# Paired heads on the two column halves of TensorE in the 64-wide attentions of a two-block transformer kernel

## What is computed

```python
# first block, for each of 8 query heads h (two key/value heads, four query heads on each)
o_cmp = softmax(q_h @ kc.T) @ vc          # 31 compressed keys
o_slc = softmax(q_h @ k_slc.T + alibi_h) @ v_slc   # causal; the selection takes in every block here
o_win = softmax(q_h @ k_win.T + alibi_h) @ v_win   # causal; the window is as long as the sequence
o_nsa = g0 * o_cmp + g1 * o_slc + g2 * o_win
# second block, for each of 8 heads, one shared key and value head
o = softmax(where(selected, q_h @ k.T + bias_h, -inf)) @ v     # v is 512 x 64
```

## Time and profile before

| what | us |
|---|---|
| median of 3 runs | 1196.96 |
| span of the profiled execution, first to last instruction | 1194.5 |
| median less span (what lies around it) | 2.5 |
| PE busy | 1142.2 (96% of the span) |
| POOL, DVE, ACT busy | 496.7, 470.4, 470.3 |
| mean granted TensorE clock | 0.986 |

### The profile page before, as it was taken

One profiled execution on the slowest core, in us unless ns is written; L12 is line 12 of the kernel. 1 busy time (PEld: TensorE's weight loads), 2 busy tenths in 40 slices (PEclk: granted clock), 3 DMA queues, 4 the chain that ended last, 5 costly groups with the idle time before them and its releaser, 6 DMA issues.

```text
span 1194.5 us, 13900 instructions
## 1 busy us (share of the span) xinstructions
PE 1142.2 (96%) x5380; PEld 910.6 (76%) x5380; DVE 470.4 (39%) x971; ACT 470.3 (39%) x776; POOL 496.7 (42%) x222
## 2 busy tenths in 40 slices
PE   5999999898999989999999899998999999999996
PEld 4777778676776877788888678887888888878785
DVE  3574410387743231893520593713000000024544
ACT  6322332577765352522332673325212221223333
POOL 4331344654543523144434583442344434434441
PEclk9999999989999999999999899999999999999998
DMA  6324422000000623132332102232332332232321
GB/s 218 106 71 141 122 83 94 1 1 1 1 2 1 211 63 106 36 102 76 105 106 97 45 2 71 71 106 71 106 97 79 105 105 85 90 105 74 120 71 71
DMA packets 82480, 96.14 MB, mean 80 GB/s; under 512 B 8056, under 2 KB 66640, under 8 KB 82424
## 3 DMA queue, kind: packets, MB, share of 16 engines
q1 hardware_dynamic: 81864, 93.27, 24.6%
q0 software_dynamic: 560, 2.12, 0.5%
HBM read 93.26 MB, written 2.12 MB: 80 GB/s over the span
## 4 chain that ended last, share of the span: by engine, by line
PE 88%; DMA 3%; DVE 2%; ACT 2%; issue 2%; POOL 1%; SPq 1%; DVEq 0%; ACTq 0%; POOLq 0%
PE bank L1397 47%; PE bank L1454 21%; PE bank L1541 5%; PE bank L1500 5%; PE bank L1521 3%; DMA raw<-in_w_in 3%; PE bank L1650 1%; PE bank L1414 1%; PE bank L1478 1%; PE bank L1613 1%; POOL w_lo L627 1%; SPq L572 1%; PE bank L1576 1%; PE bank L1539 1%; PE bank L1533 1%
## 5 line engine op out<-in xcount | busy, mean ns | idle before, releaser
L627 POOL TENSOR_TENSOR w_lo<-raw,w_hi 128x2048 fp32r<-128x2048 f32 (+3 forms) x59 | 263.8, 4472 | 423.8 <-ACT w_hi L721 423.8
L1397 PE MATMUL bank<-h_hi,w_hi 128*128 128x512 f32 (+2 forms) x904 | 354.4, 392 | 1.5 <-POOL w_lo L627 1.4
L1397 PE MATMUL bank<-h_hi,w_lo 128*128 128x512 f32 (+2 forms) x904 | 352.0, 389 | 0.0
L1397 PE MATMUL bank<-h_lo,w_hi 128*128 128x512 f32 (+2 forms) x904 | 352.0, 389 | 0.0
L1397 PEld LDWEIGHTS bank<-h_hi,w_hi 128*128 128x128 f32 (+2 forms) x904 | 169.3, 187 | 39.0 <-POOL w_lo L627 1.8
L1397 PEld LDWEIGHTS bank<-h_lo,w_hi 128*128 128x128 f32 (+2 forms) x904 | 169.3, 187 | 36.3 <-issue 1.0
L1397 PEld LDWEIGHTS bank<-h_hi,w_lo 128*128 128x128 f32 (+2 forms) x904 | 169.3, 187 | 35.8
L721 ACT ACTIVATE w_hi<-raw 128x2048 fp32r<-128x2048 f32 (+3 forms) x59 | 109.8, 1861 | 208.4 <-PE bank L1454 138.5
L701 POOL TENSOR_TENSOR w_lo<-raw,w_hi 128x2048 fp32r<-128x2048 f32 x22 | 101.3, 4606 | 147.7 <-ACT w_hi L980 74.2
L1454 PE MATMUL bank<-w_hi,h_hi 128*128 128x512 f32 x368 | 144.6, 393 | 4.9 <-DVE h_lo L1269 2.5
L1454 PE MATMUL bank<-w_hi,h_lo 128*128 128x512 f32 x368 | 143.8, 391 | 0.0
(11 more groups left out here) (175 smaller groups left out, 1155.2 us busy)
## 6 DMA issues: line engine op xcount, KB each, us to landing
raw<-in_w_in SPq DMA_DIRECT2D x31, 1024.0 KB, 5.3
raw<-in_w_ffn_gate SPq DMA_DIRECT2D x11, 1024.0 KB, 5.3
raw<-in_w_ffn_up SPq DMA_DIRECT2D x11, 1024.0 KB, 5.3
raw<-in_w_out SPq DMA_DIRECT2D x8, 1024.0 KB, 5.1
raw<-in_w_ffn_down SPq DMA_DIRECT2D x8, 1024.0 KB, 5.0
raw<-in_cmp_w SPq DMA_DIRECT2D x4, 1024.0 KB, 5.7
raw<-in_w_ffn_down SPq DMA_DIRECT2D x4, 768.0 KB, 4.4
xres<-in_x SPq DMA_DIRECT2D x4, 512.0 KB, 4.9
```

Of the source, the lines that this page charges most:

```text
L627: nc.gpsimd.tensor_tensor(w_lo[:, s % 2, 0:size], raw[:, u.n % 2, 0:size], w_hi[:, s % 2, 0:size].bitcast(F32), ALU.subtract).then_inc(lo_ ...
L1397: ins = mm(dst, w_pair[w], h_pair[h], start=start and p == 0, stop=stop and p == 2)
```

## The change

The jobs of two heads of a group alternate: job 2m is of the even head and job 2m + 1 of the odd head, with the same branch and tile. In `nsa` a group is now compressed, compressed, then for each branch w = 1, 1, 2, 2, 3, 3, 4, 4. In `dsa` it is w = 1, 1, 2, 2, 3, 3, 4, 4.

PE issues the value products of a pair together, one matmul of the even head (output partitions 0 to 63) and one of the odd head (64 to 127) in turn, at the step where those of the second job stood. Those of the first job move one step back. The ring `PT` has a name for its size and keeps its three slots. PE asks for the stacks of two heads at a time, at steps 0, 8, 16 and 24 of `dsa`, and ACT's early split waits for the logits of a whole group. `diff` keeps its order.

```diff
+PRING = 3
...
-                for h in range(NSA_HEADS):
-                    kv = h // GROUP
-                    jobs.append(dict(g=h // 2, i=NT - 1, h=h, br=-1, subs=[], v=[vc[:, kv, :]]))
-                    for br in range(2):
-                        for i in range(NT):
...
+                for g in range(NSA_HEADS // 2):
+                    kv = 2 * g // GROUP
+                    for h in (2 * g, 2 * g + 1):
+                        jobs.append(dict(g=g, i=NT - 1, h=h, br=-1, subs=[], v=[vc[:, kv, :]]))
+                    for br, i, h in itertools.product(range(2), range(NT), (2 * g, 2 * g + 1)):
...
-                for h in range(DSA_HEADS):
-                    for i in range(NT):
+                for g, i in itertools.product(range(DSA_HEADS // 2), range(NT)):
+                    for h in (2 * g, 2 * g + 1):
...
-                    sc.wait_ge(s_done, attention["dsa"][NT * m + NT - 1]["r"] + 1)
+                    sc.wait_ge(s_done, attention["dsa"][2 * NT * (m // 2) + 2 * NT - 1]["r"] + 1)
...
-                            rows = slice(DH * (job["h"] % 2), DH * (job["h"] % 2) + DH)
-                            if not job["subs"]:
-                                ins = mm(O[rows, :], job["v"][0], pt, start=True, stop=False, skip_group_check=True)
-                            for j in range(i + 1 if job["subs"] else 0):
-                                ins = mm(O[rows, P * i:P * i + P], job["v"][j], pt[:, P * j:P * j + P],
...
+                    if 0 <= k - lag - 2 and which != "diff" and (k - lag) % 2 == 1:
+
+                        two = jobs[k - lag - 3:k - lag - 1]
+                        i, G = two[0]["i"], two[0]["G"]
+                        O = bank[O_BANKS[G % 2]]
+                        pe.wait_ge(pt_done, two[1]["n"] + 1)
...
+                        for j in range(1 if compressed else i + 1):
+                            for half, job in enumerate(two):
+                                rows, pt = slice(DH * half, DH * half + DH), PT[:, job["n"] % PRING, :]
+                                if compressed:
+                                    ins = mm(O[rows, :], job["v"][0], pt, start=True, stop=False, skip_group_check=True)
+                                else:
+                                    ins = mm(O[rows, P * i:P * i + P], job["v"][j], pt[:, P * j:P * j + P],
+                                             start=which == "dsa" and j == 0, stop=j == i and (which == "dsa" or job["br"] == 1),
+                                             skip_group_check=True)
+                                if j == i or compressed:
+                                    ins.then_inc(pv_done, 1)
...
-                if k in (0, 4):
-                    pe.wait_ge(first_stacks_done, 2 + k // 4)
-                elif k % 4 == 0 and k < len(attention["dsa"]):
-                    pe.wait_ge(stack_lo_done, stacked("dsa", 2 + k // 4))
+                if k == 0:
+                    pe.wait_ge(first_stacks_done, 3)
+                elif k % 8 == 0 and k < len(attention["dsa"]):
+                    pe.wait_ge(stack_lo_done, stacked("dsa", 3 + k // 4))
```

More of the change, by code:

```diff
@@ L1 @@
+import itertools
 import math
@@ L275, in build @@
         L = sb("L", [P, LRING, T])
-        PT = sb("PT", [P, 3, T])
+        PT = sb("PT", [P, PRING, T])
         st = sb("st", [P, 256])
@@ L475, in jobs_of @@
                                      select=pm_of(i))]
-                        jobs.append(dict(g=h // 2, i=i, subs=subs, h=h, br=0, v=[v2[:, j, :] for j in range(i + 1)]))
+                        jobs.append(dict(g=g, i=i, subs=subs, h=h, br=0, v=[v2[:, j, :] for j in range(i + 1)]))
             return jobs
@@ L833, in attend @@
                         sc.wait_ge(tr_done, n + 1)
-                        if n >= 3:
-                            sc.wait_ge(pv_done, n - 2)
-                        act_fn(PT[0:rows, n % 3, 0:w], t_bank(n)[0:rows, 0:w], ACT.Copy).then_inc(pt_done, 1)
+                        if n >= PRING:
+                            sc.wait_ge(pv_done, n - PRING + 1)
+                        act_fn(PT[0:rows, n % PRING, 0:w], t_bank(n)[0:rows, 0:w], ACT.Copy).then_inc(pt_done, 1)
                     if which == "diff" and 0 <= k - lag - 2 and jobs[k - lag - 2]["last"]:
@@ L1523, in attend @@
                         ins.then_inc(tr_done, 1)
-                    if 0 <= k - lag - 2:
+                    if 0 <= k - lag - 2 and which == "diff":
                         job = jobs[k - lag - 2]
-                        i, G, pt = job["i"], job["G"], PT[:, job["n"] % 3, :]
+                        i, G, pt = job["i"], job["G"], PT[:, job["n"] % PRING, :]
                         O = bank[O_BANKS[G % 2]]
@@ L1530, in attend @@
                             pe.wait_ge(o_free, G - 1)
-                        if which == "diff":
-                            for j in range(i + 1):
-                                ins = mm(O[:, P * i:P * i + P], pt[:, P * j:P * j + P], job["v"][j], start=j == 0,
-                                         stop=j == i)
-                        else:
-                            rows = slice(DH * (job["h"] % 2), DH * (job["h"] % 2) + DH)
-                            if not job["subs"]:
-                                ins = mm(O[rows, :], job["v"][0], pt, start=True, stop=False, skip_group_check=True)
-                            for j in range(i + 1 if job["subs"] else 0):
-                                ins = mm(O[rows, P * i:P * i + P], job["v"][j], pt[:, P * j:P * j + P],
-                                         start=which == "dsa" and j == 0, stop=j == i and (which == "dsa" or job["br"] == 1),
-                                         skip_group_check=True)
@@ L1544, in attend @@
-                        ins.then_inc(pv_done, 1)
+                        for j in range(i + 1):
+                            ins = mm(O[:, P * i:P * i + P], pt[:, P * j:P * j + P], job["v"][j], start=j == 0,
+                                     stop=j == i)
+                        ins.then_inc(pv_done, 1)
+                    if 0 <= k - lag - 2 and which != "diff" and (k - lag) % 2 == 1:
[3 more added lines that the diff above has]
+                        pe.wait_ge(pt_done, two[1]["n"] + 1)
+                        if G >= 2 and (k - lag - 3 == 0 or jobs[k - lag - 4]["last"]):
+                            pe.wait_ge(o_free, G - 1)
+                        compressed = not two[0]["subs"]
+                        for j in range(1 if compressed else i + 1):
[9 more added lines that the diff above has]
+                                    ins.then_inc(pv_done, 1)
```

8 lines of the change are left out of this document (4 added, 4 removed).

## The result

The changed kernel takes 1178.56 us (median of 4 runs, 1175.75 to 1184.13) against 1197.74 us (4 runs, 1196.86 to 1200.04) for the kernel before on the same chip: ratio 0.984, 95% interval 0.982 to 0.986. The direction was forecast, the size was not: 19 us instead of 29, and the time is 0.6 us above the range of 1156 to 1178.

The account below looks back on a forecast made before the run. PE was taken to bound nsa, with DVE and POOL nearly full in most of dsa. Savings of 25.4 us in nsa and 4 in dsa, 29.4 together, gave 1167.5 us against 1196.96, range 1156 to 1178.

Parts of the forecast that it names:

- What bounds: PE bounds nsa until ACT's or DVE's work is reached; in dsa DVE and POOL are nearly full.
- Streaming: Paired heads' value products overlap fully on column halves: PE saves 17.6 us in nsa, 8.8 in dsa, compressed products 3.6.
- only neighbours overlap: Rival for value products: strict program order leaves each pair one step more than half; 1172.5 us, chance 0.12.
- Entering and leaving: Halving the blocks of value products saves their 0.34 us of gaps each: 12.2 us in nsa, 5.4 in dsa.
- nsa by group: Each nsa group set by its fullest engine plus about 1 us of waits: 80.2 us instead of 105.6, saving 25.4.
- The ring: ACT's copy into PT waits for the pair's block; its 0.85 us fits while ACT is under 0.6 us behind.
- dsa: Saves 4 us, mainly in the last stretch with PE alone, ending near 719 instead of 723.5 us; bounds 0 to 8.
- The lost clock: Rival: PE's new pauses lower its clock through dsa and lose the gain there; 1171.5 us, chance 0.03.
- The signs: Pairs take 0.7 us (w = 2) and 1.1 (w = 4), nsa 86, dsa 49; ACT or DVE fullest in nsa's first two groups.
- No overlap: Rival: column halves share what they need, only gaps go, 12.2 us in nsa, about 3 in dsa; 1182 us, chance 0.06.
- PE as the bound: Rival: ACT and DVE fill their gaps without loss, saving 33.4 + 7 us; 1156.5 us, chance 0.08.
- The ping-pong: Rival: late ACT makes pair, copy and next pair follow one another, 52 us lost against 47.6 gained; 1201 us, chance 0.04.

Follow-up runs that it names:

- e3: Changed kernel with a pair's two inner loops swapped, so all of one head's records come before the other's; 1180.3 us, nsa 93.7 us.
- e4: Changed kernel with both heads of a pair put on columns 0 to 63, loops still alternating; 1192.3 us, nsa 104.1 us.
- e6: Changed kernel with DVE's bias addition in dsa (L1148) left out; 1165.0 us, dsa 42.6 us.
- e7: Changed kernel with POOL's early low parts and its stacks of heads 3 to 7 narrowed to 8 columns; 1173.1 us, dsa 48.2 us.
- e9: Kernel before the change with DVE's bias addition in dsa left out; 1193.9 us, dsa 48.8 us.
- e15: Changed kernel with the normalisation reordered: root behind the last exponential, DVE's pieces spread, same output; 1173.7 us, nsa 85.2 us.
- e8: Changed kernel with DVE's pieces of the normalisation behind the first attention narrowed to 8 columns; 1170.5 us, nsa 83.8 us.

## Why the prediction was right and wrong, step by step

**What bounds.** Right for `nsa`: all of the gain is there, and where PE bounds the third group it fell by 8.0 us. For `dsa` "two engines that are nearly full" was read rightly from the earlier trace rows but not carried through to the end of the stage.

**Streaming.** Right. Full overlap was chosen from L1551 against L1561, and the sixteen records take 1.09 us as forecast. The rule of the Trainium skill (TensorE: Matmul & The Clock Gate, "The mechanism" of packing small matmuls), that matmuls start and end in program order, stood behind the rival in which only neighbours overlap (chance 0.12). By it e3, where only two records of a pair are neighbours on different halves, should have been nearly as long as e4: some 1.85 us for sixteen. It took 1.58, and 0.66 where e4 took 1.09. The traces don't agree with the rule for these products.

**Entering and leaving.** Right where PE bounds: 3.1 us forecast for a group, 2.9 to 3.0 measured with e4 in the second and third.

**nsa by group.** Forecast 21.3, 21.8, 19.6 and 17.5 us, 80.2 in all; measured 23.8, 22.0, 18.9 and 18.6, 83.3. This is the step that failed in `nsa`. The second group was right (DVE's 20.6 us and a little more). For the first I took ACT's 20.5 us of work as its length plus 1 us of waits. A sum of busy time doesn't say how the work is spaced: of ACT's 20.5 us, 1.6 stand in one piece in front of a copy that PE needs (table load and root; the second load, 1.3 us, comes 2 us later), PE has no work in hand for that long, and the low clock after its wait comes on top, 3.1 us in all. In the third group there were no such waits, in the fourth PE waits for ACT's copies in front of two of the last pairs (0.30 and 0.74 us); a fourth buffer makes the group 0.9 us shorter.

**The ring.** Right in the first three groups of `nsa`, where it costs nothing; the fourth loses 0.9 us by it. PE waits for `PT` before 9 of the 36 pairs of `nsa`, so not at most of them.

**dsa.** This is the larger miss: 4 us forecast, 0.6 lost. The step that failed is "In the last stretch PE is alone". Its sum let DVE have four jobs and a copy, some 6 us, behind POOL's extra work. The trace of before has seven jobs and the copy there, from the end of POOL's L646 at 707.9 us to 717.9, with only 0.16 us of waiting for PE:

```profile
706.19 1.74 POOL L646 TENSOR_TENSOR h_lo<-zs,h_hi 128x512 fp32r<-128x512 f32 x1
708.08 0.40 DVE L1146 TENSOR_TENSOR L<-bank,pool 128x256 f32<-128x256 f32 x1
...
713.38 0.42 DVE L1146 TENSOR_TENSOR L<-bank,pool 128x256 f32<-128x256 f32 x1 [0.16 <-PE bank L1500]
...
717.23 0.69 DVE L1148 CUSTOM_DVE_ANT_0 L<-L,pool 128x512 f32<-128x512 f32 x1
```

With these 10 us and the 5.5 for what follows, which were right (5.6 after), the same sum ends at 723.4 us instead of 719: no gain. The 8.5 us of DVE in the 14.5 us of the last stretch hid this, because DVE is done 5.5 us before its end. In the changed kernel seven jobs follow POOL's last L648 too, and DVE starts its last minimum 46.9 us after the start of the stage, 46.5 before. So the chain through DVE and POOL is as long as it was and PE's saving only made PE wait. e6, e7 and e9 show this by emptying DVE or POOL. e6 and e9 also show that the 6 us are there once DVE gives way.

**The lost clock.** Listed as a rival for `dsa` with 0.03 and taken to lie inside the range. It is real, in `nsa` behind the root and in `dsa` in several places. It alone did not decide, but it adds to both misses; it should have been priced as a consequence of every place in which PE goes from bound to not bound.

**The sum and the range.** The median is 11.1 us above the forecast: 3.5 us are `nsa`, 4.6 `dsa`. The other 3 us are no step of the prediction: 0.8 is the kernel before, whose median was 1197.74 with one more run, and the stages that the change doesn't touch were longer (5.4 us in the profiled execution). The range was also narrower than its own terms. Waits of 3 us instead of 1 in four groups are 8 us and no gain in `dsa` is 4, which makes 1179.5 us and not 1177.

**The signs.** The pairs took the times that were named. `nsa` was not 86 us but 91, `dsa` not 49 but 53, and in the first group PE was the fullest engine (20.9 us, ACT 19.5), partly by its low clock; in the second it was DVE, as forecast.

**The other rivals.** No overlap, 1182 us, is nearest to the measured time but for another reason: e4 is what it describes, at 1192. PE as the bound needed the pieces and the root out of the way: e15 has it in `nsa` (85.2 us; forecast for that rival 79.7). The ping-pong didn't come.

## What to carry to other kernels

The small products here overlap fully on separate column halves, and putting two blocks together saves the gaps around them: measure both apart, by putting them on the same half. When the bound engine gets lighter, look for the longest single piece on the next ones, not for their sum: a root with its table loads that cost nothing under a full PE cost 3.1 us in the change. Follow the next engine to its last instruction of the stage, not only by its share of a stretch. Before pairing work in a stage, empty the second-fullest engine in the kernel as it is: here the stage shortened from 52.7 to 48.8 us, and a lighter PE then gained nothing by itself.

## What the runs showed of the hardware

- Records on the other half of the columns overlap not only as neighbours: with four of one head ahead the pair is fully overlapped (0.66 us), with eight ahead it saves 0.38 of 0.87 us (e3 against e4).
- Entering and leaving a block of half-width products shows 0.17 us each way with nothing to wait for: nine blocks fewer in a group of `nsa` were worth 2.9 to 3.0 us.
- After one wait of 1.93 us PE ran at a granted clock of 0.60 for the next 4 us; after waits of 0.57 and 1.19 us at 0.66 over 5 us. A wait of 1.68 us in e8, at the place of the first, was followed by the full clock.
- DVE's minimum of a 128x128 tile, with all operands in SBUF, takes 0.29 us alone and 0.77 in the mean in `dsa`, up to 1.04 when it begins behind a scaling of POOL. With its logits from PSUM it takes 0.29 in the mean (e6). Making POOL lighter took 3.9 us off DVE's 43.2 without changing one of its instructions.
